# A hybrid decoder trunk on one core: the causal mask added by TensorE, maximum and exponent read from the bank, and the inputs of the compression in half as many adds

## The chip, the core and the metric

The kernel runs on one core of one Trainium2 chip. The metric is the time of one execution on the device, in microseconds. The engines are named as the profile names them: PE is TensorE's matrix product, PEld its weight load, DVE is VectorE, ACT is ScalarE, POOL is GpSimd, SP is SyncE, which only issues transfers here.

## The reference

256 tokens of width 1024 pass two layers. A layer has a mixer (attention in three branches, a convolution, a pooling), a cross-attention over 256 memory tokens, and experts that are looked up by product keys: each token takes 16 experts in each of 8 heads, 128 rows of u and v of 16384. The change touches the mixer's attention alone. Cut to it:

```python
q, kc, ks, kw = _rope(q, pos), _rope(kc, pos), _rope(ks, pos), _rope(kw, pos)
# compressed branch: blocks of 32 tokens, 16 apart, each plus a position code, through a small MLP
blk = t[:, cidx] + pe[None, None, :, None, :]
k_cmp = gelu(blk @ w1) @ w2                                  # the same for v_cmp
s_cmp = einsum('bskgd,bnkd->bkgsn', qg, k_cmp) * scale       # scale = 64 ** -0.5
p_cmp = where(valid_cmp, softmax(where(valid_cmp, s_cmp, NEG)), 0)
# selected branch: with 256 tokens all 4 blocks of 64 are selected, so it is causal attention on ks, vs
s = einsum('btkgd,bktnld->bkgtnl', qblk, kg) * scale
p = softmax(where(kpos <= tpos, s, NEG));  o_sel = p @ vg
# window branch: a window of 512 over 256 tokens is causal attention too, on kw, vw
o = g0 * o_cmp + g1 * o_sel + g2 * o_win                     # 8 query heads, 2 heads of keys and values, width 64
```

## The kernel before

Tokens are worked in two tiles of 128 (a token is a partition), so there are 2 x 2 = 4 dense parts (layer, tile). The program has five stages. The first (0 to 228 us) does the dense part of layer 0, tile 0, and the projections of the memory. Each of the next three does the next dense part and, between its steps, the experts of the part before. The last one does experts alone. Second and fourth stage have tile 1 with 256 keys, first and third have tile 0 with 128 keys (`own_half`).

**The stream of experts.** For each of the 128 expert slots of a token POOL gathers one row of u and v for every token, 1 MB in all (`gather`, L486), into one of ten slots. VectorE takes the dot product (L527), ScalarE its gelu (L994) and scales a diagonal block with it (L1000), TensorE adds gate x row (L1257) to an accumulator, and this frees the slot for POOL's next gather. Two rows are a batch. In the first stage no stream runs; POOL starts it when the first experts are known.

**The order.** A list of steps (`PLAN`, `MEM_PLAN` for the second stage, `FIRST_PLAN` for the first) sets the same order of steps on every engine, and `spread` puts batches of experts between them. Each engine's queue is worked in this order. TensorE's steps write into four banks of 2 KB a partition in turn: a job opens a bank only when the job four places earlier is drained (`open_job`, `drain`, `wait_drained`). The weights come in blocks of 2 MB through a ring of two (more places in the first stage), loaded by SP when their place is free.

**The steps around the change.** `turn_kv`: ScalarE copies transposed keys and queries from banks into `kv_t` and `q_t` (L1038 is the line of all such copies). `cmp_in` (L696): VectorE adds the position code to the keys and values of the compression, 16 operations on 64 partitions; TensorE's `cmp_hidden` (L1398) reads them. `sel_scores` and `win_scores`: TensorE multiplies the queries of a head with its keys, 64 rows high, eight heads; they fill 2 banks (jobs SS0, SS1 or SW0, SW1, 4 heads each) in tile 0 and 4 banks (2 heads each) in tile 1. VectorE then, job by job, scales and adds the mask, from bank to SBUF (L719), which drains the bank, and takes the negative maximum (L726). `sel_exps` and `win_exps`: ScalarE takes the exponent of each head with its sum (L1114). Then TensorE transposes the weights (L1279), ScalarE copies them, and `sel_values` multiplies them with the values (job OS, `kv_n,area` in the rows). VectorE's `sel_out` (L767) takes OS out of its bank.

Of the kernel before, what the change touches and what calls it, by code (L numbers as in the profile page):

```python
# [66 lines left out]
for _name, _w in (("causal", S), ("cadd", NC), ("cvalid", NC), ("cur", 4 * P), ("prev", 4 * P), ("flag", 1)):  # L67
    TC[_name] = (_n, _w)
    _n += _w
# [130 lines left out]
def build_program(nc, a):  # L200
    with ExitStack() as ctx:
# [96 lines left out]
        def stage(dense, experts, mem_layer=None, first=False, last=False):  # L298
# [43 lines left out]
            def bank_of(job):  # L342
                return bank[at[job] % BANKS]
# [61 lines left out]
            with nc.Block(no_gpsimd_drain=not last) as block:  # L405
# [113 lines left out]
                def _(dve):  # L519
# [162 lines left out]
                    def cmp_inputs():  # L682

                        dve.wait_ge(sems["k_turned"], 1)
                        at_pe, _ = SMALL["pe"]
                        for kind in range(2):
                            for kvh in range(KV_HEADS):
                                rows = slice(kvh * HD, (kvh + 1) * HD)
                                for half in range(2):
                                    out = cmp_in[half * HD:(half + 1) * HD, kind, :, kvh * NC:(kvh + 1) * NC]  # L690
                                    for hi in range(2):

                                        tok = kv_t[rows, kind, hi * CMP_STRIDE:hi * CMP_STRIDE + S].rearrange(
                                            "p (n c e) -> p c n e", c=8, e=2)[:, :, :, half]
                                        pe_at = at_pe + kind * 32 + half * 16 + hi * 8
                                        v.tensor_tensor(  # L696
                                            out[:, hi * 8:hi * 8 + 8, :], tok,
                                            smalls[rows, pe_at:pe_at + 8].unsqueeze(2).to_broadcast([HD, 8, NC]),
                                            ALU.add).then_inc(sems["cmp_in_built"], 1)
# [13 lines left out]
                    def score_pairs(prefix, signal):  # L713
                        for i in range(score_jobs):
# [25 lines left out]
                    def cmp_scores():  # L740
                        for i in range(2):
                            job = f"SC{i}"
                            wait_filled(dve, job)
                            ins = v.scalar_tensor_tensor(
                                out=p_cmp[:, 4 * i:4 * i + 4, :],
                                in0=bank_of(job)[:, 0:4 * NC].rearrange("p (h n) -> p h n", h=4),
                                scalar=HD ** -0.5, in1=tile_const("cadd").unsqueeze(1).to_broadcast([P, 4, NC]),
                                op0=ALU.mult, op1=ALU.add)
# [27 lines left out]
                    def win_scores():  # L776
                        wait_filled(dve, f"TS{score_jobs - 1}")
                        score_pairs("SW", "win_scored")
# [208 lines left out]
                def _(act):  # L987
# [122 lines left out]
                    def exp_heads(scored, done, col):  # L1110
                        for i in range(score_jobs):
                            act.wait_ge(sems[scored], i + 1)
# [608 lines left out]
```

## Time and profile before

| what | value |
| --- | --- |
| median of 3 runs | 1818.84 us (1818.31 to 1820.25) |
| the profiled execution | 1820.68 us, its span 1818.9 us |
| busy, share of the span | PE 75%, PEld 38%, DVE 62%, ACT 27%, POOL 37% |
| moved | 701.65 MB, mean 386 GB/s; gathers 536.90 MB of it |
| experts start (L532, one for each stage with experts) | 228.7 us the first, 1486.6 us the last |
| one load of the tile's constants (`tcon`) | 656.5 KB, four loads |

Shares of busy time are means over stages with different limits. So read the slices and stretches first, then the timelines of those stretches. In a timeline row stand the start, the busy time of a group (overlapping passes, so starts are better than durations for TensorE), engine, line, operation, output and inputs, shape and count, and in brackets the idle time before it and what ended it. 64\*128 in a TensorE row is the part of the array used: 64 rows by 128 columns.

### The profile page before, as it was taken

To read this page: it belongs to the slowest core of one execution; us is meant where nothing else is said; L and a number is where in the kernel's file an instruction comes from. 1 tells how busy PE (TensorE), PEld (TensorE's weight loads), DVE (VectorE), ACT (ScalarE), POOL (GpSimd) and SP (SyncE) were. 2 spreads that over 40 slices of the span, in tenths; PEclk is the share of its full clock that TensorE was granted. 3 is DMA by queue.
4 is the path that set the end of the run, shared out by engine and by line. 5 is a ranking of instruction groups with operands and counts; after the bars stand their busy time and mean duration, and the time that the engine had idled before them with its cause. 6 is when DMAs were issued, how large, how long until landed. Compare 5 with 4: busy or idle time off the path is not lost. (4 is left out here: it accounts for less than half of the span.)

```text
span 1818.9 us, 22650 instructions
## 1 busy us (share of the span) xinstructions
PE 1355.5 (75%) x8276; PEld 690.4 (38%) x8276; DVE 1129.5 (62%) x2791; ACT 483.5 (27%) x1283; POOL 671.1 (37%) x1028
## 2 busy tenths in 40 slices
PE   8999886668989958576888868576888865566554
PEld 5855842233663633222354533233363521111111
DVE  5520589885332567988544667987554578954544
ACT  3411231353211331124332232124342122211111
POOL 0000224334323433444433434343443445555451
PEclk9999988679989988887889879786999876786786
DMA  9742699999989999999999999999999999999996
GB/s 399 285 172 92 280 420 422 374 357 373 422 342 397 422 420 421 423 423 420 422 423 422 422 383 425 420 423 421 398 424 422 422 396 396 395 422 421 421 422 268
DMA packets 87518, 701.65 MB, mean 386 GB/s; under 512 B 10096, under 2 KB 10224, under 8 KB 12144
## 3 DMA queue, kind: packets, MB, share of 16 engines
q0 software_dynamic: 73728, 536.90, 71.7%
q1 hardware_dynamic: 13680, 163.32, 21.8%
q8 instruction: 65, 1.06, 0.2%
q14 instruction: 45, 0.37, 0.0%
HBM read 698.09 MB, written 2.10 MB: 385 GB/s over the span
## 5 line engine op out<-in xcount | busy, mean ns | idle before, releaser
L486 POOL DMA_INDIRECT uv_rows<-uv_in,idx x512 | 509.4, 995 | 1097.8 <-PE acc_pe L1257 841.9
L1257 PE MATMUL acc_pe<-uv_rows,diag 64*64 64x512 f32 x4096 | 627.9, 745 | 346.9 <-ACT diag L1000 333.1
L527 DVE CUSTOM_DVE_ANT_0 uv_rows<-uv_rows,h_ps 128x1024 f32<-128x1024 f32 x512 | 606.8, 1218 | 251.2 <-DMA uv_rows<-uv_in,idx 239.4
L1257 PEld LDWEIGHTS acc_pe<-uv_rows,diag 64*64 64x64 f32 x4096 | 159.3, 158 | 724.1 <-ACT diag L1000 492.7
L994 ACT ACTIVATE gelu_b<-act_b 128x2 f32<-128x2 f32 x256 | 51.8, 202 | 816.9 <-DVE act_b L527 794.1
L1284 PE MATMUL bank<-w_ring,h_t 128*128 128x512 f32 x400 | 182.2, 610 | 13.3 <-DMA w_ring<-blocks_in 11.0
L1284 PEld LDWEIGHTS bank<-h_t,w_ring 128*128 128x128 f32 x1600 | 182.4, 193 | 22.2 <-issue 19.6
L1284 PE MATMUL bank<-h_t,w_ring 128*128 128x128 f32 x1600 | 186.8, 278 | 2.1 <-DMA w_ring<-blocks_in 1.2
L480 POOL TENSOR_TENSOR diag<-ident_st,gate 128x64 f32<-128x64 f32 x512 | 161.4, 316 | 14.3 <-DVE gate L938 5.1
L1000 ACT ACTIVATE diag<-diag,gelu_b 128x64 f32<-128x64 f32 x512 | 150.2, 340 | 8.5 <-issue 0.2
L1284 PEld LDWEIGHTS bank<-w_ring,h_t 128*128 128x128 f32 x400 | 75.8, 194 | 120.1 <-issue 99.7
L1038 ACT ACTIVATE area<-bank 128x512 f32<-128x512 f32 (+1 forms) x73 | 42.1, 577 | 245.8 <-PE bank L1284 206.0
L820 DVE TENSOR_TENSOR xs<-xs,bank 128x512 f32<-128x512 f32 x16 | 11.0, 687 | 154.3 <-PE bank L1284 154.3
L655 DVE SCALAR_TENSOR_TENSOR conv<-hc,smalls,conv 128x128 f32<-128x128 f32 x240 | 66.3, 352 | 0.1
L1279 PE MATMUL bank<-ident,area 128*128 128x128 f32 x208 | 31.6, 301 | 29.1 <-ACT area L1013 13.5
L994 ACT ACT_TABLE_LOAD x40 | 51.3, 1283 | 1.6
L1279 PEld LDWEIGHTS bank<-ident,area 128*128 128x128 f32 x208 | 26.4, 156 | 43.5 <-issue 16.2
L527 DVE DVE_READ_ACCUMULATOR2_ANT act_b<- 128x1 f32 x512 | 41.9, 82 | 0.0
L559 DVE TENSOR_TENSOR h_t<-bank,smalls 128x512 f32<-128x512 f32 x24 | 15.8, 688 | 33.9 <-PE bank L1279 29.1
L1284 PE MATMUL bank<-area,w_ring 128*128 128x256 f32 x128 | 31.4, 407 | 7.4 <-DMA area<-mem_gained 7.4
L834 DVE TENSOR_REDUCE st<-bank 128x2 f32<-128x512 f32 x8 | 5.5, 692 | 49.8 <-PE bank L1284 49.7
L1565 PE MATMUL acc_pe<-xs,zero 128*128 128x512 f32 x16 | 14.1, 1030 | 26.1 <-PEq L1604 26.1
(218 smaller groups left out, 1219.2 us busy)
## 6 DMA issues: line engine op xcount, KB each, us to landing
w_ring<-blocks_in SPq DMA_DIRECT2D x62, 2048.0 KB
uv_rows<-blocks_in SPq DMA_DIRECT2D x9, 2048.0 KB, 15.0
uv_rows<-uv_in,idx POOLq DMA_INDIRECT x512
tcon<-tile_consts_in SPq DMA_DIRECT2D x4, 656.5 KB, 10.6
uv_rows<-blocks_in SPq DMA_DIRECT2D x2, 1024.0 KB, 7.0
h_ffn<-ffn_gain_in SPq DMA_DIRECT2D x4, 512.0 KB
xs<-x_in SPq DMA_DIRECT2D x2, 512.0 KB, 17.6
uv_rows<-mem_in SPq DMA_DIRECT2D x1, 1024.0 KB, 13.5
```

What stands on the lines that cost most here:

```text
L480: nc.gpsimd.tensor_tensor(diag[:, slot_of(k), :], ident_st[:, :], gate[:, k:k + 1].to_broadcast([P, HT]), ALU.mult).then_inc(sems["gates_s ...
L486: nc.gpsimd.indirect_dma_start(uv_rows[:, slot_of(k), :, :].rearrange("p a n -> p (a n)"), None, a["uv"], bass.IndirectOffsetOnAxis(ap=idx ...
L527: v.tensor_tensor_reduce(u_row, u_row, h_ps[:, :], 1.0, 0.0, ALU.mult, ALU.add, act_b[:, k // B % AHEAD, k % B:k % B + 1]).then_inc(sems[" ...
L559: ins = v.tensor_tensor(h_t[:, 4 * i:4 * i + 4, :], bank_of(job)[:, :].rearrange("p (c t) -> p c t", c=4), small(gain, 4 * i, 4).unsqueeze ...
L655: ins = v.scalar_tensor_tensor(out=conv[:, g, :], in0=hc[:, g, k:k + P], scalar=small("cw", g * CONV_W + k, 1), in1=conv[:, g, :], op0=ALU ...
L994: s.activation(gelu_b[:, b % AHEAD, :], act_b[:, b % AHEAD, :], ACT.Gelu_apprx_tanh).then_inc(sems["gelu_done"], 1)
L1000: s.activation(diag[:, slot_of(k), :], diag[:, slot_of(k), :], ACT.Copy, scale=gelu_b[:, b % AHEAD, k % B:k % B + 1]).then_inc(sems["diag_ ...
L1038: drain(s.activation(out, src, func, **kw), job)
L1257: mm = pe.matmul(acc_pe[c * HT:(c + 1) * HT, r * BLK:(r + 1) * BLK], diag[tok, slot_of(k), :], uv_rows[tok, slot_of(k), 1, c * BLK:(c + 1) ...
L1279: mm = pe.transpose(out[:, i * P:(i + 1) * P], src, ident[:, :])
L1284: mm = pe.matmul(out, lhs, rhs, start=(i == 0), stop=(i == len(pairs) - 1))
L1565: pe.matmul(acc_pe[:, c * 512:(c + 1) * 512], zero[:, :], xs[:, 0:512], start=True, stop=False, skip_group_check=True)
```

## The change

Three things change.

The mask. The scores are no longer scaled and masked by VectorE. The queries are scaled by 64 ** -0.5 in their copy from the bank, and TensorE adds the mask: behind each head's product it multiplies the identity with a 128 x 128 causal mask into the last 128 columns of the same output. The mask constant shrinks from 256 columns to 128. The scores of the compressed branch keep VectorE's add, without the scale.

Who reads the bank. VectorE takes the maximum from the bank, and ScalarE takes the exponents from the bank into SBUF. So the bank is drained by the last exponent of the job, and ScalarE waits for this exponent to end before it counts it as done.

The inputs of the compression. Keys and values go together in one operation, 8 operations of 2 x 8 x 16 elements in place of 16 of 8 x 16.

```diff
-for _name, _w in (("causal", S), ("cadd", NC), ...
+for _name, _w in (("causal", P), ("cadd", NC), ...
...
-                        for kind in range(2):
-                            for kvh in range(KV_HEADS):
...
-                                for half in range(2):
-                                    out = cmp_in[half * HD:(half + 1) * HD, kind, :, kvh * NC:(kvh + 1) * NC]
...
+                        for kvh in range(KV_HEADS):
+                            rows = slice(kvh * HD, (kvh + 1) * HD)
+                            pe_rows = small("pe").rearrange("p (k e c) -> p k e c", k=2, e=2)[rows]
+                            for half in range(2):
+                                out = cmp_in[half * HD:(half + 1) * HD, :, :, kvh * NC:(kvh + 1) * NC]
...
                             wait_filled(dve, job)
-                            ins = v.scalar_tensor_tensor(
-                                out=probs[:, h0:h0 + n, 0:keys],
-                                in0=bank_of(job)[:, :].rearrange("p (h k) -> p h k", h=n), scalar=HD ** -0.5,
-                                in1=tile_const("causal", 0, keys).unsqueeze(1).to_broadcast([P, n, keys]),
-                                op0=ALU.mult, op1=ALU.add)
-                            drain(ins, job)
-                            wait_drained(dve, job)
-                            v.tensor_reduce(st[:, 8 + h0:8 + h0 + n], probs[:, h0:h0 + n, 0:keys], AX.X, ALU.max,
+                            v.tensor_reduce(st[:, 8 + h0:8 + h0 + n],
+                                            bank_of(job)[:, :].rearrange("p (h k) -> p h k", h=n), AX.X, ALU.max,
                                             negate=True).then_inc(sems[signal], 1)
...
-                        copy_bank(q_t[:, :, :], "QT", "q_turned", view=c_t(4))
+                        copy_bank(q_t[:, :, :], "QT", "q_turned", view=c_t(4), scale=HD ** -0.5)
...
+                    def exp_heads(prefix, scored, done, col):
                         for i in range(score_jobs):
+                            job = f"{prefix}{i}"
                             act.wait_ge(sems[scored], i + 1)
...
+                            for k, h in enumerate(job_heads(i)):
+                                ins = s.activation(probs[:, h, 0:keys], bank_of(job)[:, k * keys:(k + 1) * keys],
+                                                   ACT.Exp, bias=st[:, 8 + h:9 + h],
+                                                   accum_out=st[:, col + h:col + h + 1])
+                                if k < score_heads - 1:
+                                    ins.then_inc(sems[done], 1)
+                            drain(ins, job)
+                            wait_drained(act, job)
+                            act.sem_inc(sems[done], 1)
...
+                    def masked_scores(out, h, kind):
+
+                        pe.matmul(out, q_t[head_rows(h), h % 4, :], kv_t[head_rows(h), kind, 0:keys], start=True,
+                                  stop=False)
+                        return pe.matmul(out[:, keys - P:keys], ident[:, :], tile_const("causal"), start=False,
+                                         stop=True)
```

The order of instructions moves at three places. On TensorE, in the first stage, behind the compression's first layer (`L1398`, `uv_rows,area2`), the eight score products stood together. Before:

```order
L1398 MATMUL bank0<-uv_rows,area2 32x256 [waits w_landed2,w_landed3,bank_drained0,cmp_in_built]
L1398 MATMUL bank0<-uv_rows,area2 32x256 x31
L1284 MATMUL bank1<-kv_t,q_t 128x128 [waits bank_drained1,bank_drained2,k_turned,q_turned]
L1284 MATMUL bank2<-kv_t,q_t 128x128
L1284 MATMUL bank1<-kv_t,q_t 128x128
L1284 MATMUL bank2<-kv_t,q_t 128x128
```

and now each has a mask product (`tcon,ident`) behind it, and the heads of the two banks alternate as they did:

```order
L1397 MATMUL bank0<-uv_rows,area2 32x256 x31
L1429 MATMUL bank1<-kv_t,q_t 128x128 [waits bank_drained1,bank_drained2,k_turned,q_turned]
L1431 MATMUL bank1<-tcon,ident 128x128
L1429 MATMUL bank2<-kv_t,q_t 128x128
L1431 MATMUL bank2<-tcon,ident 128x128
L1429 MATMUL bank1<-kv_t,q_t 128x128
```

Eight products have become sixteen in turn; what stands before and behind them is the same.

On TensorE, in the second stage, the last window job, a batch of experts, and then the product of selection weights and values (`kv_n,area2`). Before:

```order
L1284 MATMUL bank0<-kv_t,q_t 128x256 [waits bank_drained0]
L1284 MATMUL bank0<-kv_t,q_t 128x256
L1257 MATMUL acc_pe<-uv_rows,diag 64x512 [waits diag_done]
L1257 MATMUL acc_pe<-uv_rows,diag 64x512 x3
L1257 MATMUL acc_pe<-uv_rows,diag 64x512 [waits diag_done]
L1257 MATMUL acc_pe<-uv_rows,diag 64x512 x3
L1284 MATMUL bank1<-kv_n,area2 128x64 [waits bank_drained1,v_kept,sel_turned]
L1284 MATMUL bank1<-kv_n,area2 128x64 x15
```

and now:

```order
L1431 MATMUL bank0<-tcon,ident 128x128
L1256 MATMUL acc_pe<-uv_rows,diag 64x512 [waits diag_done]
L1256 MATMUL acc_pe<-uv_rows,diag 64x512 x3
L1256 MATMUL acc_pe<-uv_rows,diag 64x512 [waits diag_done]
L1256 MATMUL acc_pe<-uv_rows,diag 64x512 x3
L1283 MATMUL bank1<-kv_n,area2 128x64 [waits bank_drained1,v_kept,sel_turned]
L1283 MATMUL bank1<-kv_n,area2 128x64 x15
```

The place of the last product has not moved: one batch behind the window scores, in bank 1, the bank of the first window job. What empties bank 1 before it has moved from VectorE to ScalarE. In ScalarE's queue the window exponents of that stage now read banks (`area1` is the SBUF tile of the weights):

```order
L1107 ACTIVATE area1,st<-bank1,st 128x256 [waits win_scored]
L1107 ACTIVATE area1,st<-bank1,st 128x256
L1107 ACTIVATE area1,st<-bank2,st 128x256 [waits bank_drained1,win_scored]
L1107 ACTIVATE area1,st<-bank2,st 128x256
L1107 ACTIVATE area1,st<-bank3,st 128x256 [waits bank_drained2,win_scored]
```

Their number and place are as before; the waits for the job's last exponent are new, and each bank is released here.

## Rows read from the trace of the kernel before

**Rows 1.** The page: mean busy share of the 16 DMA engines in 40 slices of the span.

```profile
DMA  9742699999989999999999999999999999999996
```

**Rows 2.** Timeline of POOL, 190 to 232 us: start, duration, instruction, [idle before <- releaser].

```profile
201.21 1.11 POOL L486 DMA_INDIRECT uv_rows<-uv_in,idx  x1 [200.76 <-SPq L405]
```

**Rows 3.** Timeline of PE, first stage (columns as in group 2).

```profile
51.46 7.15 PE L1284 MATMUL bank<-uv_rows,w_ring 128*128 128x256 f32 x32
58.54 3.66 PE L1398 MATMUL bank<-uv_rows,area 128*32 128x256 f32 x64
62.13 1.16 PE L1284 MATMUL bank<-kv_t,q_t 64*128 64x128 f32 x16
63.23 0.66 PE L1406 MATMUL bank<-ident_kind,area 128*128 128x64 f32 x4
63.72 7.12 PE L1284 MATMUL bank<-uv_rows 128*128 128x256 f32 x32
70.78 0.42 PE L1284 MATMUL bank<-hid_k,smalls 128*64 128x16 f32 x8
...
76.54 2.08 PE L1284 MATMUL bank<-kv_t,q_t 64*128 64x128 f32 x16 [1.75 <-DVE conv_u L793]
78.55 9.28 PE L1284 MATMUL bank<-uv_rows 128*128 128x256 f32 x32
```

**Rows 4.** Stretches: busy us (instructions) of PE, PEld, DVE, ACT, POOL; clock; DMA share; GB/s.

```profile
76.00:83.00 7.00, 6.46 (x27) 5.42 (x28) 4.48 (x11) 4.09 (x17) 0.00 (x0) 0.51 0.01 5
...
340.00:380.00 40.00, 30.23 (x215) 13.73 (x208) 36.34 (x92) 16.27 (x46) 15.54 (x25) 0.70 1.01 417
380.00:410.00 30.00, 22.69 (x155) 12.46 (x157) 24.32 (x53) 15.68 (x40) 11.82 (x18) 0.83 0.88 322
...
800.00:900.00 100.00, 77.79 (x509) 32.26 (x502) 77.55 (x176) 40.36 (x115) 47.77 (x72) 0.80 1.01 422
...
1270.00:1290.00 20.00, 16.16 (x120) 9.15 (x119) 15.12 (x28) 11.19 (x22) 10.32 (x16) 0.90 0.93 366
```

**Rows 5.** Waits of DVE, 340 to 440 us, the longest: us in total, times, longest.

```profile
DVE xs L820 <- PE bank L1284: 9.8, 1, 9.8
```

**Rows 6.** Waits of DVE, 800 to 900 us, the longest.

```profile
DVE uv_rows L527 <- DMA uv_rows<-uv_in,idx: 8.9, 9, 1.3
```

**Rows 7.** Timeline of PE, later in the first stage.

```profile
129.04 14.45 PE L1284 MATMUL bank<-h_t,uv_rows 128*128 128x128 f32 x128
...
147.79 7.03 PE L1284 MATMUL bank<-w_ring,uv_rows 128*128 128x512 f32 x16
154.65 1.04 PE L1279 MATMUL bank<-ident,area 128*128 128x128 f32 x8
```

**Rows 8.** Timeline of DVE, second stage.

```profile
363.84 0.69 DVE L726 TENSOR_REDUCE st<-area 128x2 f32<-128x512 f32 x1
...
385.22 0.69 DVE L719 SCALAR_TENSOR_TENSOR area<-bank,tcon 128x512 f32<-128x512 f32 x1 [1.59 <-PE bank L1284]
...
389.90 0.69 DVE L726 TENSOR_REDUCE st<-area 128x2 f32<-128x512 f32 x1
...
397.65 0.69 DVE L767 TENSOR_TENSOR area<-bank,st 128x512 f32<-128x512 f32 x1
...
406.54 0.43 DVE L788 BATCH_NORM_STATS2 st<-bank 128x6 f32<-128x256 f32 x1 [2.73 <-PE bank L1279]
```

**Rows 9.** Timeline of DVE, first stage: the inputs of the compression.

```profile
49.27 5.35 DVE L696 TENSOR_TENSOR area<-kv_t,smalls 64x128 f32<-64x128 f32 x16 [4.99 <-ACTq L1041]
```

**Rows 10.** Timeline of PE, second stage.

```profile
383.98 2.10 PE L1284 MATMUL bank<-kv_t,q_t 64*128 64x256 f32 x16
...
387.88 3.79 PE L1284 MATMUL bank<-kv_n,area 128*128 128x64 f32 x32
```

**Rows 11.** Timeline of ACT, second stage: the first window exponent.

```profile
395.03 0.51 ACT L1114 ACTIVATE area<-area,st 128x256 f32<-128x256 f32 x1
```

**Rows 12.** Timeline of PE, fourth stage.

```profile
1264.93 7.09 PE L1284 MATMUL bank<-kv_n,area 128*128 128x64 f32 x32
```

More of the change, by code:

```diff
@@ L66 @@
 _n = 0
-for _name, _w in (("causal", S), ("cadd", NC), ("cvalid", NC), ("cur", 4 * P), ("prev", 4 * P), ("flag", 1)):
+for _name, _w in (("causal", P), ("cadd", NC), ("cvalid", NC), ("cur", 4 * P), ("prev", 4 * P), ("flag", 1)):
     TC[_name] = (_n, _w)
@@ L684, in cmp_inputs @@
                         dve.wait_ge(sems["k_turned"], 1)
-                        at_pe, _ = SMALL["pe"]
-                        for kind in range(2):
-                            for kvh in range(KV_HEADS):
-                                rows = slice(kvh * HD, (kvh + 1) * HD)
-                                for half in range(2):
-                                    out = cmp_in[half * HD:(half + 1) * HD, kind, :, kvh * NC:(kvh + 1) * NC]
[L691 to L699, printed above, removed]
+                        for kvh in range(KV_HEADS):
[3 more added lines that the diff above has]
+                                out = cmp_in[half * HD:(half + 1) * HD, :, :, kvh * NC:(kvh + 1) * NC]
+                                for hi in range(2):
+                                    tok = kv_t[rows, 0:2, hi * CMP_STRIDE:hi * CMP_STRIDE + S].rearrange(
+                                        "p k (n c e) -> p k c n e", c=8, e=2)[:, :, :, :, half]
+                                    v.tensor_tensor(
+                                        out[:, :, hi * 8:hi * 8 + 8, :], tok,
+                                        pe_rows[:, :, half, hi * 8:hi * 8 + 8].unsqueeze(3).to_broadcast(
+                                            [HD, 2, 8, NC]), ALU.add).then_inc(sems["cmp_in_built"], 1)
                     def cmp_kv():
@@ L743, in cmp_scores @@
                             wait_filled(dve, job)
[L744 to L748, printed above, removed]
+                            ins = v.tensor_tensor(
+                                p_cmp[:, 4 * i:4 * i + 4, :],
+                                bank_of(job)[:, 0:4 * NC].rearrange("p (h n) -> p h n", h=4),
+                                tile_const("cadd").unsqueeze(1).to_broadcast([P, 4, NC]), ALU.add)
                             drain(ins, job)
@@ L1390, in cmp_hidden @@
                     def cmp_hidden():
[L1391 removed]
+                        pe.wait_ge(sems["cmp_in_built"], 8)
                         out = open_job("HID")
@@ L1435, in scores @@
                                     h = 4 * i + k
-                                    mm = product(outs[i][:, k * P:(k + 1) * P],
-                                                 [(q_t[head_rows(h), k, :], kv_t[head_rows(h), kind, 0:P])])
+                                    mm = masked_scores(outs[i][:, k * P:(k + 1) * P], h, kind)
                                     if k == 3:
@@ L1443, in scores @@
                             for k, h in enumerate(job_heads(i)):
-                                mm = product(out[:, k * S:(k + 1) * S],
-                                             [(q_t[head_rows(h), h % 4, :], kv_t[head_rows(h), kind, 0:S])])
+                                mm = masked_scores(out[:, k * S:(k + 1) * S], h, kind)
                             close_job(mm, f"{prefix}{i}")
@@ L1628, in constants @@
         tok = tile * P + t
-        put(tile, "causal", np.where(np.arange(S)[None, :] <= tok[:, None], 0.0, NEG))
+        put(tile, "causal", np.where(t[None, :] <= t[:, None], 0.0, NEG))
         n = np.arange(NC)
```

12 lines of the change are left out of this document (4 added, 8 removed).

## The prediction

> **What bounds the kernel now.** I read four views. First the page's row of the DMA engines by slice [rows 1]: from the sixth slice to the last but one it stands at 9 nearly throughout, while slices 2 to 5 (45 to 227 us) show 7, 4, 2, 6. So the kernel has two regimes: a first stage in which nothing streams, and then the stream of expert rows. Second, the queue that starts the stream: POOL issues its first gather at 201.21 us [rows 2]. All that delays this instruction delays the end by as much, since what follows is 1600 us of transfers that share one bandwidth.
>
> Third, the timeline of TensorE in the first stage [rows 3]. Between 51.46 and 74 us its groups touch: each starts where the one before ends, and the next row with an idle time is that of 76.54 (1.75 us, for a bank that VectorE empties). TensorE is therefore the engine on the path here; VectorE and ScalarE have waits between their pieces. After 78.55 a projection of 9.28 us runs, and short dependent steps follow.
>
> Fourth, the stretches [rows 4]. In the second stage, 340 to 380 us, the DMA share is 1.01, but from 380 to 410 it is 0.88 at 322 GB/s, and VectorE's list of waits from 340 to 440 holds no wait for a landed row; its longest is one for TensorE [rows 5]. So there the chain of VectorE, ScalarE and TensorE sets the pace and the transfers follow. In the third stage (800 to 900 us) the share is 1.01 and VectorE's longest wait is for landed rows, 8.9 us [rows 6]: there the transfers set the pace. The fourth lies between: full, with one dip to 0.93 at 1270 to 1290 us [rows 4].
>
> **The masks on TensorE.** Each head's product gets a second one behind it, identity by mask, 128 columns over all 128 rows. In the trace one float32 product is two passes (eight score products stand as x16). A full-height pass of 128 columns takes 14.45 / 128 = 0.113 us, and 16 passes of 512 columns start 6.86 us before the next group, 0.84 ns a column, 0.107 us for 128 columns [rows 7]. The masks alone are 16 x 0.113 = 1.8 us in each score step.
>
> The scores themselves get dearer too. Today 16 passes of 128 columns on 64 rows take 1.10 us from start to start (62.13 to 63.23), half of what 16 x 0.107 = 1.7 would give [rows 3]: passes of the upper and lower rows run beside each other. A mask between any two uses all rows, so I expect this to stop, and 32 passes to cost 32 x 0.107 = 3.4 us.
>
> Then the change of shape. 32 passes of 256 columns are as many columns as 16 of 512. Followed by a group of the same shape, such a block lasts 6.86 us (147.79 to 154.65) [rows 7]; followed by one that uses another part of the array it lasts 7.08 (51.46 to 58.54) and 7.06 us (63.72 to 70.78) [rows 3]. I read the 0.2 us between them as the price of one change of shape. The changed kernel alternates 64-row and 128-row products, two changes a head, 16 a step: 3.2 us. A score step in the first stage is then 3.4 + 3.2 = 6.6 us against 1.10, +5.5. Bounds: +1.8 (masks alone, pairing kept, changes free); +2.5 with the pairing lost and changes free (32 x 0.113 = 3.6); +7.3 if a change costs 0.3. I take 5.5: the two blocks with 0.2 are the nearest rows to such a change, and they agree.
>
> The Trainium skill bears on this, in "TensorEngine Tiling (Array Packing)", Key Properties: changing the tiling mode, and not only the tile, drains TensorE. It gives no figure. By that rule the sum comes out where I put it, near 1836; with changes of shape free it comes out near 1827 (the first rival). The starts above agree with it as far as they go.
>
> There are two such steps in the first stage, selection and window: 2 x 5.5 = **+11.0 us** (bounds +3.6 and +14.6). Nothing gives it back: what TensorE does behind the first (63.23 on) needs only TensorE's turn. The second starts at half clock: from 76 to 83 us the granted clock is 0.51 [rows 4], after the idle time at 76.54. In that stretch a pass takes twice as long, but the stretch ends some 7 us after the restart whatever runs in it, so the lost time stays the same and the added work is paid at full clock behind it.
>
> What hides there: the exponents now read the bank and so hold it until they are done. In the first stage two jobs (mem_kv2 and mem_kv3, 7.1 us each at full clock) stand behind the score jobs on TensorE, longer than the eight exponents. The maximum reads a bank instead of SBUF at the same 0.69 us, by the add that reads it today [rows 8]. The adds it replaces, four of 0.69 us, sit in VectorE's slack. The inputs of the compression take 5.35 us now, 0.334 each [rows 9]; an operation of 512 elements takes 0.69 [rows 8], so on the line between them 256 elements take 0.45, 8 x 0.45 = 3.6: saves 1.7 us (bounds 0 and 2.7). It ends at 54.6, and its reader starts at 58.54 behind a projection: worth nothing in the first stage. If that cover went, it would be worth at most 1.7.
>
> **The second stage.** Here I follow the chain. The compression gives VectorE 1.7 us. The selection scores are 16 x 256 + 16 x 128 = 6144 columns, 5.1 us, and 3.2 us of changes: 8.3 us at full clock where 2.1 stands now [rows 10]. The stretch has a mean clock of 0.70 [rows 4], so they end near 366, and the four maxima near 367, where today the last ends at 364.53 [rows 8]: +2.5, even though four adds (2.7 us) are gone. The window scores start 2.5 later and take 8.3: the last is in the bank at 383.98 + 2.5 + 8.3 = 394.8, the maxima end at 395.7, today 390.6 [rows 8, 10]: +5.1. The exponents start at 395.03 + 5.1 = 400.1 [rows 11].
>
> Now the new wait. The product of selection weights and values runs at 387.88 [rows 10], in the bank of the first window job. Today that bank is free after VectorE's add at 385.22; in the changed kernel only after ScalarE's two exponents, about 401.3. TensorE's queue stands behind it: the next batch of expert products, which frees row slots for POOL. After such a pause the product runs at half clock, as in the fourth stage, 7.09 us [rows 12], or in 3.79 [rows 10]. It ends at 405.1 to 408.4, and VectorE, which reads it at 397.65 today without waiting [rows 8], waits: +7.5 to +10.8. The wait of 2.73 us that stands at 406.54 [rows 8] gives part of it back. I take **+7 us** (bounds: -4, if the score steps stay hidden and VectorE keeps what it saves; +11).
>
> **The other stages.** In the third, rows land just in time [rows 6], and ten slots are under way, some 25 us of transfers, more than the 5.5 us that TensorE is late: 0. In the fourth the product of selection and values has a batch more ahead of it and starts at 1264.93 [rows 12], after the exponents as it is; 2.7 + 2.7 + 1.7 us less on VectorE can at most fill the dip, 7% of 20 us, 1.4 us [rows 4], and the longer scores take it back: 0 (bounds -1.5 and +3). The mask constant shrinks by 128 columns in each of four loads, 64 KB at the 422 GB/s of [rows 4], 0.16 us, three of them in the stream: **-0.5**.
>
> Sum: 11.0 + 7 - 0.5 = +17.5 us. The profiled execution took 1820.68 us (span 1818.9), so 1838.2; it lies 1.8 above the median of the runs, 1818.84. Against that median: 1836.
>
> **Rivals.**
> First, changes of shape cost nothing. For it: the 0.2 us is seen only at the ends of long groups. Then +2.5 a step, 5.0 in the first stage; in the second the window scores end 2 us later and the bank wait remains, +3.5: with -0.5, 1827.
> Second, it comes out even: the wait for the bank lands in time that the transfers need anyway (share 1.01 until 380), and the first stage costs its lower bound, 3.6, against 1 to 3 us gained: 1820.
> Third, faster: VectorE's relief decides. It is busy 36.34 of 40 us from 340 to 380 [rows 4], and loses 8 x 0.69 + 1.7 = 7.2 us in the second stage. If the whole of it counts, the fourth gives 1.4, the constant 0.5, and the first stage costs 3.6: -5.5, 1813. It decides when a masked step in the first stage costs less than 4.5 us and TensorE keeps up with VectorE in the second; against it stand the touching groups of [rows 3].
> Fourth, much slower: slots freed 6 to 14 us late in the second stage make VectorE wait for rows, or the clock stays low where TensorE's work is now so broken up: +30, 1849.
>
> **How the numbers follow.** Forecast (+12 to +25) 0.50; no price for changes 0.24; even 0.10; faster 0.10; much slower 0.06. A measurement of this kernel tells about 0.2%, 3.6 us, from no change. Slower is 0.50 + 0.24 + 0.06 = 0.80, same 0.10, faster 0.10. The range takes the forecast and the first rival with their bounds: 1822 to 1845.
>
> **What would show it.** In the changed trace: between the group at 62.13 and the gelu's transposes 6.6 us instead of 1.10 (3.6 if the first rival holds); the first gather at 212 (206); the selection product in the second stage with TensorE idle ahead of it until the first two window exponents are done, and VectorE's multiplication behind it waiting; no wait for TensorE of such kind in the third. The prediction is wrong if the masked step costs under 4 us, or if the second stage's wait is swallowed.

## The result, and the profile after

The changed kernel takes 1845.84 us (median of 4 runs, 1839.61 to 1847.92), the kernel before 1819.55 (4 runs, 1818.31 to 1821.38) beside it: a ratio of 1.0136, 95% interval 1.0121 to 1.0152 (the two medians by themselves give 1.0144). The forecast was 1836, with 1845 as its upper end, from a base of 1818.84; that base times the ratio is 1843.6, while the bare median lies 0.8 above the upper end. The profiled execution took 1847.92 us, span 1846.0, against 1820.68 and 1818.9: +27.1 in the span. The page's row of DMA slices shows where to look: of the weak slices 2 to 5 of [rows 1] three are lower still (6, 3, 2, 5 for 7, 4, 2, 6), and slices 9 and 10 (369 to 462 us) fell from 9 to 7.

```profile
DMA  9632599977989999999999999999999999999996
```

The start of each stage's experts is marked by VectorE's copy of h_ps (four in a trace). The time between two such marks is a stage's length:

| stage ends at (us) | first | second | third | fourth | rest of the span |
|---|---|---|---|---|---|
| before | 228.67 | 672.84 | 1080.50 | 1486.58 | 1818.9 |
| changed | 241.29 | 700.34 | 1108.42 | 1514.62 | 1846.0 |
| length, changed less before | +12.6 | +14.9 | +0.4 | +0.1 | -0.9 |

So the loss has the two places that were forecast, and no third; both are larger. POOL's first gather, against [rows 2], is 14.87 us later; 12.6 of them are left when the experts start. (From the gather to that start it is 25.2 us here and 27.5 before, and 25.3 to 28.0 in the traces of the experiments, so I read the difference as the spread of executions.)

```profile
216.08 1.11 POOL L486 DMA_INDIRECT uv_rows<-uv_in,idx  x1 [215.63 <-SPq L405]
```

TensorE's timeline of the first stage, against [rows 3]:

```profile
59.85 3.66 PE L1397 MATMUL bank<-uv_rows,area 128*32 128x256 f32 x64
63.44 0.49 PE L1429 MATMUL bank<-kv_t,q_t 64*128 64x128 f32 x2
63.86 0.49 PE L1431 MATMUL bank<-tcon,ident 128*128 128x128 f32 x2
...
69.69 0.49 PE L1431 MATMUL bank<-tcon,ident 128*128 128x128 f32 x2
70.02 0.56 PE L1405 MATMUL bank<-ident_kind,area 128*128 128x64 f32 x4
...
83.23 0.77 PE L1429 MATMUL bank<-kv_t,q_t 64*128 64x128 f32 x2 [1.75 <-DVE conv_u L783]
83.93 0.79 PE L1431 MATMUL bank<-tcon,ident 128*128 128x128 f32 x2
...
94.05 0.79 PE L1431 MATMUL bank<-tcon,ident 128*128 128x128 f32 x2
94.64 8.06 PE L1283 MATMUL bank<-uv_rows 128*128 128x256 f32 x32
102.54 0.27 PE L1278 MATMUL bank<-ident,p_cmp 128*128 128x128 f32 x1
```

Read the starts of the groups. A head's score and its mask, two passes each of 128 columns, come 0.415 us apart (63.44, 63.86). Two passes stream in 2 x 0.107 = 0.21 us; I read the other 0.20 us as the change of shape, which the experiments test. The selection step goes from 63.44 to 70.02, 6.58 us, against 1.10. The window step lasts from 83.23 to 94.64, 11.41 us against 2.01: there the same groups stand 0.72 apart. The stretches show the clock at which this ran (columns as in [rows 4]); the last row is of the second stage:

```profile
76.00:83.00 7.00, 5.48 (x50) 4.72 (x48) 2.16 (x7) 4.01 (x7) 0.00 (x0) 1.00 0.06 27
83.00:90.00 7.00, 6.77 (x19) 4.78 (x20) 1.02 (x5) 0.92 (x2) 0.00 (x0) 0.50 0.00 0
...
95.00:103.00 8.00, 8.00 (x37) 6.89 (x36) 1.06 (x3) 2.44 (x13) 0.00 (x0) 0.90 0.01 2
...
370.00:380.00 10.00, 10.00 (x24) 5.46 (x22) 2.58 (x8) 3.67 (x6) 0.46 (x2) 0.50 1.00 420
```

The granted clock is 0.50 (1.2 GHz) from the restart after the idle 1.75 us until past 95 us, and back at full only beyond that (a mean of 0.90 from 95 to 103). In the kernel before, the low clock of [rows 4] was over by 83 us: the stretch from 83 to 85 us has 1.00. The 14.87 us at the gather are then: 5.48 for the selection step, 9.40 for the window step, 1.31 that TensorE already came late (59.85 against 58.54), less 1.22, since mem_kv3 behind the window step lasts 8.06 us from 94.64 on and 9.28 in [rows 3]. That is 0.10 too much, and the 0.10 lies between the two steps (13.21 us from 70.02 to 83.23, where 13.31 stood). The 1.31 us go along with a load of blocks at the start whose issue took 1.47 us in place of 0.43. It took between 0.77 and 1.80 us in the traces of the experiments, 1.09 in that of the kernel before with nothing but its order changed, so I read it as the spread of executions and not as part of the change; that it makes TensorE late by just so much is not shown.

TensorE in the second stage, against [rows 10]:

```profile
370.17 0.79 PE L1431 MATMUL bank<-tcon,ident 128*128 128x128 f32 x2
370.90 1.22 PE L1429 MATMUL bank<-kv_t,q_t 64*128 64x256 f32 x2
...
383.29 0.79 PE L1431 MATMUL bank<-tcon,ident 128*128 128x128 f32 x2
...
404.34 0.70 PE L1429 MATMUL bank<-kv_t,q_t 64*128 64x256 f32 x2
...
412.27 0.49 PE L1431 MATMUL bank<-tcon,ident 128*128 128x128 f32 x2
...
419.10 6.20 PE L1283 MATMUL bank<-kv_n,area 128*128 128x64 f32 x28 [4.46 <-ACT area L1107]
```

The selection scores run from 369.02 to 384.0, 15 us, at half clock throughout (0.50 in each stretch from 366 to 384), where they took 5.0 before (355.69 to 360.66), at half clock too. TensorE's rows and a stretch of the kernel before:

```profile
356.53 4.20 PE L1284 MATMUL bank<-kv_t,q_t 64*128 64x256 f32 x14
360.66 2.95 PE L1257 MATMUL acc_pe<-uv_rows,diag 64*64 64x512 f32 x16
```

```profile
356.00:360.00 4.00, 4.00 (x19) 3.30 (x18) 3.86 (x10) 1.71 (x4) 0.00 (x0) 0.50 0.99 418
```

The window scores take 8.35 us at full clock (404.34 to 412.69), as forecast (8.3). Then TensorE stands idle for 4.46 us, released by ScalarE's exponents, and the product of selection and values runs at half clock, as forecast (6.20 us in this row, which lacks four of its passes). VectorE against [rows 8]:

```profile
384.12 0.69 DVE L717 TENSOR_REDUCE st<-bank 128x2 f32<-128x512 f32 x1 [3.06 <-PE bank L1431]
...
412.80 0.69 DVE L717 TENSOR_REDUCE st<-bank 128x2 f32<-128x512 f32 x1 [1.40 <-PE bank L1431]
...
426.27 0.69 DVE L758 TENSOR_TENSOR area<-bank,st 128x512 f32<-128x512 f32 x1 [5.57 <-PE bank L1283]
```

The last selection maximum ends at 384.8 (364.53 before), the last window maximum at 413.5 (390.6), and the multiplication behind the product starts at 426.27, now with a wait of 5.57 us, where [rows 8] has it at 397.65 without one: +28.6, of which 12.6 were there when the stage began. The fourth stage has the same steps: there both ran at full clock (8.36 us each), TensorE waited 0.72 us for the bank, and the stage cost 0.1.

### The profile page after: what moved, and what is told of

Its sections match the earlier page's. It is cut to its first block and busy times, and to the rows that moved or that the text cites. A ratio compares the mean times of both kernels' runs of the same rounds, so it can differ in the third digit from the quotient of the medians.

```text
span 1846.0 us, 22874 instructions
## 1 busy us (share of the span) xinstructions
PE 1405.9 (76%) x8404; PEld 724.7 (39%) x8404; DVE 1110.0 (60%) x2735; ACT 483.6 (26%) x1283; POOL 674.2 (37%) x1028
## 5 line engine op out<-in xcount | busy, mean ns | idle before, releaser
L717 DVE TENSOR_REDUCE st<-bank 128x2 f32<-128x512 f32 (+1 forms) x24 | 16.4, 691 | 54.2 <-PE bank L1431 53.8
L1429 PE MATMUL bank<-kv_t,q_t 64*128 64x256 f32 (+1 forms) x128 | 44.4, 432 | 1.8 <-DVE conv_u L783 1.8
```

The lines of the kernel that those rows point to most:

```text
L717: v.tensor_reduce(st[:, 8 + h0:8 + h0 + n], bank_of(job)[:, :].rearrange("p (h k) -> p h k", h=n), AX.X, ALU.max, negate=True).then_inc(se ...
L1429: pe.matmul(out, q_t[head_rows(h), h % 4, :], kv_t[head_rows(h), kind, 0:keys], start=True, stop=False)
```

## The experiments

All ratios are to the kernel before, run beside each, with their 95% intervals. The code shown is cut, marked by `...`. The record of the experiments names two chips: the runs of the masks by stage and the second run of the filled idle time come from one, all others from another; the kernel before has a median of 1819.59 us on the first and of 1820.75 and 1820.58 on the other.

**One mask product for a bank.** The mask of all heads in the bank is put there first, and the scores are added to it; the same columns, few changes of shape.

```diff
-  pe.matmul(out, q_t[head_rows(h), h % 4, :], kv_t[head_rows(h), kind, 0:keys], start=True, stop=False)
-  return pe.matmul(out[:, keys - P:keys], ident[:, :], tile_const("causal"), start=False, stop=True)
+  pe.matmul(out[:, :].rearrange("p (h k) -> p h k", h=n)[:, :, keys - P:keys], ident[:, :],   # once a bank
+            tile_const("causal").unsqueeze(1).to_broadcast([P, n, P]), start=True, stop=False, ...)
+  return pe.matmul(out, q_t[head_rows(h), h % 4, :], kv_t[head_rows(h), kind, 0:keys],        # each head
+                   start=False, stop=True, ...)
```

> Theory (each change between 64-row and 128-row products costs TensorE about 0.2 us at full clock, and passes of 64 rows lose their overlap when a 128-row product stands between them): with one mask product for the whole bank ahead of its scores, a score step in the first stage has two changes in place of sixteen and its scores stand together again: 1.72 (4 passes of 512 columns) + 1.10 + 0.4 = 3.2 us in place of 6.6 at full clock, 6.2 in place of 11.4 at half. First gather near 207.5 us (changed kernel 216.08), second stage some 7 us cheaper, in all about 1831 us. Rival A (what is dear is the columns of the masks, not the changes): the columns are the same here, the steps stay at 6 us and more, and the time stays at 1845.

1831.21 us (1828.74 to 1836.38), ratio 1.0052 [1.0037, 1.0067]. TensorE in the first stage, selection and then window step:

```profile
63.66 1.98 PE L1429 MATMUL bank<-tcon,ident 128*128 128x512 f32 x4
65.57 1.16 PE L1434 MATMUL bank<-kv_t,q_t 64*128 64x128 f32 x16
66.66 0.66 PE L1405 MATMUL bank<-ident_kind,area 128*128 128x64 f32 x4
```

```profile
79.98 3.75 PE L1429 MATMUL bank<-tcon,ident 128*128 128x512 f32 x4 [1.75 <-DVE conv_u L783]
83.66 2.08 PE L1434 MATMUL bank<-kv_t,q_t 64*128 64x128 f32 x16
```

3.0 us from 63.66 to 66.66 (3.2 expected) and 5.7 for the window step at half clock. The starts show one change of shape by itself: the four mask passes take 1.91 us to the next group, 0.20 more than their columns (4 x 512 x 0.837 ns = 1.71). The first gather is at 206.44 us. Rival A falls: the columns are the same, and more than half of the loss is gone (+10.5 us on the medians, where it was +26.3). In the trace the first stage is 5.7 us over before, the second 5.3, and the fourth 4.2, which the changed kernel did not lose there; I have no cause for that last one.

**A mask product of the scores' own shape.** It leaves out the mask for half of the queries of each head, so this kernel tells about time alone.

```diff
-  return pe.matmul(out[:, keys - P:keys], ident[:, :], tile_const("causal"), ...)
+  return pe.matmul(out[:, keys - P:keys], ident[head_rows(h), :], tile_const("causal")[head_rows(h), :], ...)
```

> The mask product takes only the 64 rows of the array on which its head's scores run, so the mask of the other half of the queries is left out; number, columns and order of the products are those of the changed kernel. Theory (the change of shape is what costs): no change is left, 32 passes of 64 rows overlap as 16 do today, and the first stage's selection step takes 2 x 1.10 = 2.2 us, the window step 4 to 5 at half clock; first gather near 205, in all about 1827 us. Rival B (what costs is that a product adds to a place of the bank that the product before it has just written, or that it is so small): the 0.2 us a product stays, the step takes 2.2 + 3.2 = 5.4 us, and the time is about 1841.

1819.66 us (10 runs, 1817.88 to 1823.67), ratio 0.9996 [0.9987, 1.0005]. TensorE in the first stage, a group of mask passes, a group of score passes, and what follows the step:

```profile
63.55 0.40 PE L1431 MATMUL bank<-tcon,ident 64*128 64x128 f32 x4
63.77 0.49 PE L1429 MATMUL bank<-kv_t,q_t 64*128 64x128 f32 x4
...
65.31 0.66 PE L1405 MATMUL bank<-ident_kind,area 128*128 128x64 f32 x4
```

Such groups of four passes, scores and masks in turn, start every 0.22 us, 0.056 a pass, half of the 0.107 that one takes alone; the whole step takes 2.1 us (63.22 to 65.31). As many products, each adding to what was just written, and no 0.2 us: rival B falls. The window step was expected at 4 to 5 us, the gather near 205 and the whole at 1827; all three came out lower, and in this trace the clock did not fall in the first stage:

```profile
78.62 0.50 PE L1429 MATMUL bank<-kv_t,q_t 64*128 64x128 f32 x4 [1.75 <-DVE conv_u L783]
```

The idle time ahead is the same 1.75 us, yet the granted clock is 1.00 from 78 us on, the step takes 2.1 us (to 80.68), and mem_kv3 behind it 7.0 from start to start, where it took 9.1 before. This gives back what the selection step costs, and the first gather is at 201.24. So this kernel shows what the shape costs, not that such masks are free, and the idle time alone does not settle the clock. In the second stage the product of selection and values waits all the same:

```profile
389.35 7.06 PE L1283 MATMUL bank<-kv_n,area 128*128 128x64 f32 x32 [4.46 <-ACT area L1107]
```

**No masks at all**, the reading side alone.

```diff
-  return pe.matmul(out[:, keys - P:keys], ident[:, :], tile_const("causal"), start=False, stop=True)
```

> The masks are left out (all scores stand unmasked); maximum and exponent are still taken from the bank and the queries scaled in their copy. Theory (the first stage's loss is all mask products; in the second stage the wait of TensorE for the bank of the first window job remains and costs about what VectorE saves): score steps 1.1 and 2 us again, first gather 201.2 to 202.5, the selection product of the second stage still waits for two exponents, some 4 us, the multiplication behind it comes +2 us; in all 1818 to 1823 us. Rival C (reading from the bank is itself the loss, by exponents that hold the banks): 1828 and more. Rival D (VectorE's relief counts once the masks cost nothing): 1813.

1818.43 us (10 runs, 1814.62 to 1822.14), ratio 0.9988 [0.9979, 0.9998]. The selection step is back at 1.09 us and the window step at 2.0, the first gather at 202.38. VectorE's multiplication in the second stage:

```profile
397.77 0.69 DVE L758 TENSOR_TENSOR area<-bank,st 128x512 f32<-128x512 f32 x1 [5.61 <-PE bank L1283]
```

It starts 168.2 us into the stage, 169.0 before: what VectorE saves in adds ahead of it is lost in this wait. In the whole stage 2.9 us come out (441.25 against 444.17), of which the halved adds may be 1.8 (see the next run). So the upper bound of the whole idea in this order, with masks that cost nothing, is 0.1% on the median; rivals C and D both fall.

**The compression's inputs alone**: the kernel before with the eight adds of the diff in place of its sixteen.

```diff
-  for kind in range(2):
...
-      v.tensor_tensor(out[:, hi * 8:hi * 8 + 8, :], tok, ...)
+  v.tensor_tensor(out[:, :, hi * 8:hi * 8 + 8, :], tok, ...)          # both kinds at once
```

> The kernel before with the inputs of the compression in eight adds in place of sixteen, nothing else. Theory: 4.4 us in place of 5.35, hidden in the first stage behind TensorE's projection; within 1 us of the kernel before (1818 to 1820). Rival: it counts in the second stage's chain of VectorE, -1 us in each of the two middle stages, 1817.

1819.43 us (11 runs), ratio 0.9996 [0.9987, 1.0005]. No difference that can be measured, and none between the two theories, which lie closer than the spread. The adds take 4.41 us for 5.35. The one trace has the first stage as before, the second 1.8 us shorter (442.36) and the third as it was, so the rival's -1 in each middle stage is not what it shows either.

**Masks by stage.** The masks by TensorE and the reads from the bank only where a condition holds; elsewhere VectorE adds the mask and ScalarE reads SBUF, as before.

```diff
+  def on_pe(prefix):
+      return own_half              # second kernel: not own_half; third: prefix == "SS"
```

> Masks by TensorE and reading from the bank in the first and third stage alone; the second and fourth add their masks on VectorE as before (queries scaled in their copy everywhere). Theory (the loss has two places, the first stage's touching groups and the second stage's chain; the third stage waits for rows): first gather near 215, the first stage +12.6 us and nothing behind it, about 1832 us. Rival H (the stages are not independent: what the second stage loses comes from its late start): 1840 or more.

1834.40 us (1829.73 to 1836.48), ratio 1.0080 [1.0056, 1.0105]. First gather at 214.52; first stage +11.1 us, second -1.9, third +0.5, fourth +0.1 in the trace. That trace is of the shortest execution, as those of the next two kernels are.

> The other half: masks by TensorE in the second and fourth stage alone. Theory: first gather at 201 to 202, the second stage 459 us long in place of 444 (+15), the fourth as before; about 1834 us. Rival H: under 1826.

1835.16 us, but from 1823.57 to 1845.27 in four runs; ratio 1.0099 [1.0063, 1.0136]. The execution with the trace was the shortest, with a second stage of 448.30 us, +4.1, where +15 was expected. Both of its score steps ran at a clock of 1.00, as the first two rows show; the other two are what follows the two steps on TensorE. There is no trace of the 1845, but the mean clock that is on record for each of the four falls as the time grows: 0.870 at 1823.57, 0.866 at 1834.85, 0.863 at 1835.46, 0.851 at 1845.27.

```profile
350.00:360.00 10.00, 10.00 (x56) 5.88 (x49) 8.43 (x23) 3.66 (x6) 2.69 (x4) 1.00 1.00 425
380.00:389.00 9.00, 9.00 (x40) 4.94 (x40) 2.33 (x4) 0.79 (x3) 2.36 (x4) 1.00 0.93 377
```

```profile
360.00 1.95 PE L1278 MATMUL acc_pe<-uv_rows,diag 64*64 64x512 f32 x16
...
395.05 5.26 PE L1305 MATMUL bank<-kv_n,area 128*128 128x64 f32 x26 [4.46 <-ACT area L1129]
```

The selection step took 8.4 us here (351.62 to 360.00) against 15 in the changed kernel, with the same products. The wait of 4.46 us behind the window step is the same, though. The medians of the two halves, +14.8 and +15.6, add up to 30.4, a little more than the whole, +26.3. With ranges of 7 and 22 us this says no more than that the places are roughly independent; both medians are far from rival H's (1840 and more, under 1826), which falls.

> Masks by TensorE and reading from the bank for the selection branch in all stages; the window branch adds its masks on VectorE as before and takes its exponents from SBUF. Theory (each of the steps pays for itself; in the second stage the selection step costs +7.7 us at half clock, the window step +3 and the wait for its bank +5): first gather near 208, the second stage 7 to 9 us over before, the product of the selection's values not waiting for a bank; about 1834 us. Rival E (the bank wait costs nothing): the same kernel stays near 1838 to 1840, since only the window's own scores are saved.

1833.51 us (1827.79 to 1834.99), ratio 1.0074 [1.0052, 1.0097]. First gather at 206.13. VectorE's two multiplications in the second stage, the second without a wait:

```profile
387.44 0.69 DVE L772 TENSOR_TENSOR area<-bank,st 128x512 f32<-128x512 f32 x1 [5.05 <-PE bank L1305]
...
404.56 0.69 DVE L772 TENSOR_TENSOR area<-bank,st 128x512 f32<-128x512 f32 x1
```

It starts 172.7 us into the stage; in the changed kernel 185.0, before 169.0. The selection step ran 12.7 us here, partly at full clock, where the changed kernel's took 15.0, and cost 3.7 us at this point; leaving out the window step with its bank wait, and a selection step 2.3 shorter, took 12.3 away together. The whole second stage is 3.2 us over before, not the 7 to 9 expected; the median came out as the theory had it, and rival E's 1838 to 1840 did not.

**The order that avoids the wait.** Three kernels have the selection's values ahead of the window scores in the later stages:

```diff
- "sel_turn", "win_scores", "win_exps", "conv3", "sel_values", "sel_out", "conv_norm"
+ "sel_turn", "conv3", "sel_values", "sel_out", "win_scores", "win_exps", "conv_norm"
```

> The kernel before with that order alone, as a control: it has no wait for this bank, so the order should give nothing by theory and by rival E, 1819 to 1822; rival F: 1823 and more.

> One mask product for a bank ahead of its scores, and the order of the run before (selection's values ahead of the window scores) together. Theory: 1831 less the bank wait, 1826. Rival E: 1831. Rival F: 1834 and more.

> The changed kernel, with the product of the selection's weights and values, and VectorE's multiplication behind it, ahead of the window scores in the plans of the later stages. Theory (in the second stage the bank that this product needs is held by two window exponents, and the wait of 4.46 us on TensorE and 5.57 us on VectorE is a cost of its own): that wait is gone, and the second stage gets 4 to 6 us shorter, in all about 1841 us. Rival E (the multiplication is late only because the masked score steps ahead of it are; the bank wait costs nothing beside them): within 1 us of the changed kernel, 1845. Rival F (the order itself is worse, since VectorE now waits for the product): 1848 and more.

The control, the kernel before in this order, took 1828.85 us, 1.0048 [1.0029, 1.0067]; with one mask a bank 1831.42, 1.0060 [1.0041, 1.0078]; the changed kernel 1858.15 (1853.76 to 1868.53), 1.0223 [1.0188, 1.0258]. The theory's times (1819 to 1822, 1826 and 1841) missed in all three. Rival F holds for the order, which costs 8 us by itself, though not by the wait that it named: the control's VectorE does not wait for the product in the second stage.

```profile
389.56 0.69 DVE L767 TENSOR_TENSOR area<-bank,st 128x512 f32<-128x512 f32 x1
...
398.90 0.69 DVE L719 SCALAR_TENSOR_TENSOR area<-bank,tcon 128x512 f32<-128x512 f32 x1 [3.20 <-PE bank L1284]
...
414.30 0.16 DVE L792 RECIPROCAL st<-st 128x1 f32<-128x1 f32 x1 [7.01 <-ACT st L1133]
```

The multiplication comes early (389.56), but the window scores behind it are late, and the reciprocal of the convolution's norm waits 7 us for ScalarE. What the bank wait itself costs can only be argued from this. With one mask a bank the order costs 0.2 us where the control has it cost 8, in the second stage -0.8 against +4.3. If the order costs the same in both, some 5 us there are given back by the wait that is gone. These are single traces, though, and 1831.42 is the time that rival E gave for this kernel; in these runs it is the control alone that speaks against it. In the changed kernel the second stage became 8.4 us shorter and the fourth 11.6 longer: its selection step there ran at half clock (15.0 us for 8.4, 0.50 from 1250 to 1260), with waits of VectorE for each bank (fourth stage):

```profile
1251.29 0.69 DVE L717 TENSOR_REDUCE st<-bank 128x2 f32<-128x512 f32 x1 [2.52 <-PE bank L1431]
```

**The idle time ahead of the window scores filled**, twice.

```diff
+  if first and prefix == "SW":
+      for _ in range(10):
+          pe.matmul(h_ps[:, 0:P], ident[:, :], ident[:, :], start=True, stop=True)
```

> The changed kernel, with ten small products into a bank that nobody reads (2.3 us) put into TensorE's idle time of 1.75 us ahead of the first stage's window scores. Theory (the granted clock falls to half at that idle time and stays low through the broken-up step, so that it costs 11.4 us and not 6.6): with the idle time filled the step takes 6.6 us, the first gather comes at 210.5 to 211.5 in place of 216.08, in all about 1841 us. Rival G (the broken-up products themselves keep the clock low, whatever stands ahead of them): the clock falls inside the step all the same, first gather at 214 to 217, 1845 to 1847.

> The kernel of the filled idle time once more, for its spread (1841 to 1855 in four executions; the one with a trace had the shorter first stage and 1841) and for a second trace. Theory (the first stage is 5 us shorter each time, and what varies is at which clock the second stage's long score steps run): first gather near 211 again, with the second stage's end varying by up to 10 us. Rival G (the filling doesn't hold the clock each time): first gather near 216 in a slow execution.

1849.44 us (1840.94 to 1854.69), 1.0166 [1.0134, 1.0199], where 1841 was expected, and 1836.83 (5 runs, 1829.55 to 1839.71), 1.0087 [1.0060, 1.0114]. TensorE in the first of the two:

```profile
81.42 2.50 PE L1437 MATMUL h_ps<-ident 128*128 128x128 f32 x20
83.85 0.48 PE L1429 MATMUL bank<-kv_t,q_t 64*128 64x128 f32 x2
...
90.09 0.49 PE L1431 MATMUL bank<-tcon,ident 128*128 128x128 f32 x2
90.42 7.07 PE L1283 MATMUL bank<-uv_rows 128*128 128x256 f32 x32
```

In both traces the window step takes 6.6 us (83.85 to 90.42) and the first gather comes at 210.87 and 210.83, 5.2 earlier: the theory's step is shown, and rival G is not seen in this step. The time of the whole doesn't answer, since nine runs of one kernel lie between 1829.55 and 1854.69; the first four ran on one chip and the other five on another, and the two ranges do not overlap, so the chip may be part of it. The second trace (1830.03 us) has a second stage of 446.0 us, +1.8, and full clock in its selection step:

```profile
350.00:360.00 10.00, 9.19 (x96) 4.36 (x88) 9.97 (x32) 2.57 (x9) 7.22 (x9) 1.00 1.01 417
360.00:370.00 10.00, 9.80 (x54) 5.56 (x56) 8.32 (x20) 3.67 (x6) 2.49 (x4) 1.00 0.99 417
```

The first has 455.0 us, +10.8, with a selection step of 12.6 us, mostly at half clock. There the clock fell inside the step, as rival G has it: TensorE was idle for 2.11 us until 359.69, worked without a gap from then on, ran the first two masked heads at full clock, and then fell:

```profile
364.60 0.70 PE L1429 MATMUL bank<-kv_t,q_t 64*128 64x256 f32 x2
365.23 0.59 PE L1431 MATMUL bank<-tcon,ident 128*128 128x128 f32 x2
365.75 1.22 PE L1429 MATMUL bank<-kv_t,q_t 64*128 64x256 f32 x2
```

In the kernel with masks in the second tile alone 2.07 us of idle time stood at the same place, and the clock stayed at 1.00. So filling the idle time kept the clock up in the first stage, but what makes it fall in the second is open. I have no trace of a run near 1854 either.

## Why the prediction was right, and where its sum was short

**What bounds the kernel; the two places; nothing in the third stage.** Right. The third stage's score steps were 6.6 us too and its multiplication 6.4 us later within the stage (891.13 against 857.27), and its end moved by 0.4.

**A masked step of 6.6 us at full clock.** Right: 6.58. Both parts stood up: a change of shape costs 0.20 us (0.2 forecast, the first rival's zero is out), and without changes even masks and scores overlap, 32 passes in 2.1 us. (The upper bound, +7.3, is added up with 3.6 us of streaming; with the 3.4 of the forecast it is 7.1.)

**"The stretch ends some 7 us after the restart whatever runs in it."** This step failed. The row of [rows 4] holds one such stretch and says nothing about others. Here the low clock lasted from the restart at 83.23 until between 95 and 97 us, some 12 us and more, and the step took 11.4 inside it; with the idle time filled it took 6.6, and in the kernel with masks of 64 rows the clock did not fall at all. It cost 9.4 in place of 5.5, and the first stage +13.6 at the gather without the late load, in place of 11.0. That this lies within the bounds of +3.6 and +14.6 is luck: the upper one stood for a dearer change of shape, which did not come.

**Selection scores in the second stage "8.3 us at full clock".** Also sized at the wrong clock. They took 15.0, and the last maximum ended 7.7 us later within the stage in place of 2.5. The trace of before could have said so: the mean of 0.70 that was used is that of 40 us, while the 4 us of the step itself were granted 0.50. The second stage cost 14.9 us in place of 7, outside its bounds of -4 and +11; in traces whose steps ran at full clock it cost 1.8 and 4.1, so at that clock the 7 would have been too much.

**The new wait.** Right in kind and place: 4.46 us of idle TensorE, then half clock, then 5.57 us on VectorE. In each trace with window exponents from the bank and the old order it stands there with 4.46 to 5.28 us; it is gone in the kernel that takes only the selection's from the bank. Its price is not shown: one comparison of traces gives about 5 us, another 12.3 for it, the window step and a shorter selection step together. In the kernels without masks and with masks of 64 rows the wait stands too, and the second stage is still 2.9 and 1.9 us shorter than before, so there it costs no more than what VectorE saves.

**The fourth stage at 0.** Right here (+0.1), but it hangs on the clock: the changed order showed the same loss there, 11.6 us.

**The fourth rival.** It had 0.06 and 1849, by slots that come free late or by a clock that "stays low where TensorE's work is now so broken up". The clock is what happened, in the first stage and in the second. The measured 1845.84 is 3 us from its time and 10 from the forecast's. So the direction and the two places were foreseen; that the time still falls at the edge of the range, which was not drawn for this rival, is in part luck.

**VectorE's relief and the halved adds at nothing.** Right: 1.0 us less on the adds (4.38 for 5.35; forecast 1.7), no gain that can be measured, and 0.1% for all relief together without masks. **The constant, -0.5:** not told apart; the last part of the span was 0.9 shorter.

No kernel here beats the one before. The idea's best case, which leaves the masks out, is 0.1% faster, and the best one with all of its masks on TensorE is 0.5% slower.

## What to carry to other kernels

Before work moves to TensorE, count the changes of the array's shape that it brings, not its columns: here 0.20 us each, and one product for a bank took back some 15 of 26 us. Price a step at the clock that the step itself was granted, and take what it was granted in the longer form as open, since a step that gets longer and more broken up may lose both ways, as it did here in some executions and not in others. And when an engine is to read a bank directly, look for the job that opens this bank next: here VectorE's relief went into that wait.

## What the runs showed of the hardware

A change between 64-row and 128-row products costs TensorE 0.20 us at 2.4 GHz and 0.29 at 1.2 (groups 0.72 apart, of which 0.43 stream). The Trainium skill states in "TensorEngine Tiling (Array Packing)", Key Properties, that a change of tiling mode drains TensorE. The gaps between the groups agree with this and give it a size; the drain itself is no row of a trace. A second thing was unexpected: programs with broken-up score steps spread by 7 to 22 us within four to six executions (1823.57 to 1845.27 in one case), where the kernel before, over 48 runs, stays within 1817.13 to 1825.60. In the traces the granted clock of those steps goes along with it, but what decides it is open: after 1.75 us of idle time the clock fell in the changed kernel and stayed up in the one with masks of 64 rows.
